# Hybrid GLA and retention decoder step: retention outputs and keys turned by DMA and VectorE instead of TensorE

## The reference, cut to what matters

```python
def _layer(x, pos, s_gla, s_ret, ...):           # 2 layers, x is 2048 x 1024, fp32
    z = rmsnorm(x, norm_w) @ w_in                # one projection, columns split:
    gq, gk, gv, gg, glr, rq, rk, rv, rg = split_cols(z)      # 4 heads, dk 64, dv 128 each group
    la = log_sigmoid(glr @ w2 + b) / 16
    q_b, k_b = rope(rq), rope(rk) * 64 ** -0.5
    o_a, S_gla = gla_chunked(gq * 64 ** -0.5, gk, gv, la)    # S_t = diag(alpha_t) S + k^T v
    o_b, S_ret = ret_chunked(q_b, k_b, rv)                   # S_t = gamma_h S + k^T v
    o_a = rmsnorm_per_head(o_a) * gla_norm_w * silu(gg)
    o_b = (groupnorm_per_head(o_b) * ret_norm_w + ret_norm_b) * silu(rg)
    return x + concat(o_a, o_b) @ w_out
```

## Time and profile before

| | |
|---|---|
| median of 3 runs | 1712.52 us (1712.15 to 1712.91) |
| the profiled execution's own time | 1712.96 us |
| its span, first to last instruction | 1711.2 us |
| PE busy | 1688.4 us (99%), 10154 matmuls |
| DVE, POOL, ACT busy | 975.2, 843.8, 635.9 us |
| chain that ended last | 97% PE, of it 82% line 684 |
| granted TensorE clock | 0.999 |
| DMA | 165470 packets, 215.97 MB, 126 GB/s over the span |

### The profile page before, as it was taken

One profiled execution on the slowest core, in us unless ns is written; L12 is line 12 of the kernel. 1 busy time (PEld: TensorE's weight loads), 2 busy tenths in 40 slices (PEclk: granted clock), 3 DMA queues, 4 the chain that ended last, 5 costly groups with the idle time before them and its releaser, 6 DMA issues.

```text
span 1711.2 us, 26417 instructions
## 1 busy us (share of the span) xinstructions
PE 1688.4 (99%) x10154; PEld 1388.8 (81%) x10154; DVE 975.2 (57%) x2316; ACT 635.9 (37%) x1255; POOL 843.8 (49%) x661
## 2 busy tenths in 40 slices
PE   6999999999999999999999999999999999999998
PEld 4888878888788887888878888788887888878886
DVE  6742576746755275463754436758477454784454
ACT  4433244333343233442342423334234343343322
POOL 3445345554455544464544544547445464454635
PEclk9999999999999999999999999999999999999999
DMA  7412357433542244522454224574245422442224
GB/s 259 138 63 87 99 199 209 138 109 124 181 152 75 87 136 147 131 83 78 154 149 101 74 75 150 177 187 141 75 151 154 118 74 85 141 159 75 87 87 142
DMA packets 165470, 215.97 MB, mean 126 GB/s; under 512 B 80224, under 2 KB 82656, under 8 KB 165344
## 3 DMA queue, kind: packets, MB, share of 16 engines
q10 hardware_dynamic: 73872, 134.51, 24.0%
q1 hardware_dynamic: 91472, 79.77, 16.0%
HBM read 192.34 MB, written 21.89 MB: 125 GB/s over the span
## 4 chain that ended last, share of the span: by engine, by line
PE 97%; DMA 1%; DVE 1%; issue 0%; SPq 0%; ACT 0%; ACTq 0%; POOLq 0%; POOL 0%
PE bank L684 82%; PE bank L959 3%; PE bank L1000 2%; PE bank L965 2%; PE bank L943 1%; PE bank L926 1%; PE bank L747 1%; PE bank L905 1%; PE bank L867 1%; DMA region<-in_x_prompt 1%; PE bank L651 1%; PE bank L909 1%; PE bank L976 0%; PE bank L757 0%; PE bank L884 0%; PE bank L705 0%
## 5 line engine op out<-in xcount | busy, mean ns | idle before, releaser
L266 POOL TENSOR_TENSOR w_lo<-w_stage,w_hi 128x512 fp32r<-128x512 f32 x264 | 360.8, 1388 | 349.2 <-ACT w_hi L259 349.2
L684 PE MATMUL bank<-h_hi,w_hi 128*128 128x512 f32 x1024 | 410.2, 401 | 4.2 <-DVE h_lo L353 4.2
L684 PE MATMUL bank<-h_lo,w_hi 128*128 128x512 f32 x1024 | 400.0, 391 | 0.0
L684 PE MATMUL bank<-h_hi,w_lo 128*128 128x512 f32 x1024 | 399.8, 390 | 0.0
L266 POOL TENSOR_TENSOR w_lo<-ss,w_hi 128x512 fp32r<-128x512 f32 x164 | 218.7, 1354 | 227.8 <-ACT w_hi L259 227.8
L259 ACT ACTIVATE w_hi<-w_stage 128x512 fp32r<-128x512 f32 x264 | 152.6, 624 | 355.2 <-PE bank L684 319.7
L684 PEld LDWEIGHTS bank<-h_hi,w_hi 128*128 128x128 f32 x1024 | 192.5, 188 | 54.2 <-issue 7.2
L684 PEld LDWEIGHTS bank<-h_hi,w_lo 128*128 128x128 f32 x1024 | 192.6, 188 | 41.7
L684 PEld LDWEIGHTS bank<-h_lo,w_hi 128*128 128x128 f32 x1024 | 192.9, 188 | 36.9
L684 PE MATMUL bank<-w_hi,h_hi 128*128 128x512 f32 x512 | 202.6, 396 | 0.3 <-DVE region L1619 0.3
L684 PE MATMUL bank<-w_hi,m_hi 128*128 128x512 f32 x512 | 202.8, 396 | 0.0
(11 more groups left out here) (215 smaller groups left out, 2264.2 us busy)
## 6 DMA issues: line engine op xcount, KB each, us to landing
w_stage<-in_w_slots ACTq DMA_DIRECT2D x264, 256.0 KB, 3.0
ss<-in_w_slots ACTq DMA_DIRECT2D x164, 256.0 KB, 2.9
v_b<-in_w_slots ACTq DMA_DIRECT2D x84, 256.0 KB, 3.0
region<-in_x_prompt SPq DMA_DIRECT2D x32, 512.0 KB, 4.5
xn<-in_x_t SPq DMA_DIRECT2D x16, 512.0 KB, 4.3
out_acts<-region SPq DMA_DIRECT2D x16, 512.0 KB, 3.6
xn<-out_acts SPq DMA_DIRECT2D x128, 64.0 KB, 3.4
region<-out_acts SPq DMA_DIRECT2D x16, 512.0 KB, 3.3
```

Source lines behind the costliest of these rows:

```text
L266: pool.tensor_tensor(w_lo[:, r, c], stage(h), w_hi[:, r, c].bitcast(f32), ALU.subtract).then_inc(lo_done, 1)
L684: i = pe.matmul(P[q][:, :], x, y, start=(s == 0 and kk == 0 and c == 0), stop=(s == 3 and kk == 1 and c == 2), skip_group_check=True)
```

## The change

It takes `keys_natural` and the g = 0 half of `mixed_t` out of TensorE's stream. In their place:

- `turn_outputs` (SP, w = 14): each 128 tokens of normalised `o_n` go to DRAM (`o_rows`, 4 DMAs of 256 KB), and when all four have landed 16 DMAs of 64 KB in runs of 128 bytes bring them back, turned in blocks, into the same buffer (`o_t`). `mixed_ret` (DVE, w = 18) turns the 32x32 blocks with four transposes of 128x512, ACT applies scale and bias in place (w = 18), DVE multiplies by the gate, ACT makes `m_hi` (w = 19) and POOL `m_lo` (w = 19 to 22).
- `turn_keys` (SP, w = 6 and 18): the same for `k_t`, 2 DMAs of 256 KB out to `k_rows` and 16 of 32 KB back into `k_n`; `keys` (DVE) turns the blocks with one transpose of 128x1024, for g = 0 with a multiplication by the decay behind it.
- In blocks 3 to 6 `load_next` moves from w = 4 to 7 to w = 8 to 11, without its wait for TensorE's slot. Waits of TensorE and ACT are adapted: the first wait for `kn_sb` is now that of the states.

The core of the diff (`mixed(g, t)` of DVE loses its g = 0 half; `keys_natural` is gone):

```diff
+            def turn_outputs(n):
+                if n > 0:
+                    sp.wait_ge(ob_in.sem, ob_in.at(n, 0))
+                for t in range(TPB):
+                    sp.wait_ge(normed.sem, normed.at(n, t + 1))
+                    sp.dma_start(d["o_rows"][TOK * t:TOK * t + TOK, :], o_n[:, t, :]).then_inc(or_out.sem, 16)
+                sp.wait_ge(or_out.sem, or_out.at(n, 64))
+                for h in range(HEADS):
+                    runs = d["o_rows"][:, 128 * h:128 * h + 128].rearrange("(c b) (j a) -> j b c a", b=32, a=32)
+                    for j in range(4):
+                        sp.dma_start(o_t[32 * j:32 * j + 32, h, :].rearrange("p (c a) -> p c a", a=32), runs[j]).then_inc(ob_in.sem, 16)
+
+            def turn_keys(n, g):
+                if n > 0 or g == 1:
+                    sp.wait_ge(kb_in.sem, kb_in.at(n, 256 * g))
+                    sp.wait_ge(st_ps.sem, st_ps.at(n, 4 * g))
+                for p in range(2):
+                    sp.wait_ge(qk_gla.sem, qk_gla.at(n, 3 + p)) if g == 1 else sp.wait_ge(rope_st.sem, rope_st.at(n, 4 * p + 4))
+                    sp.dma_start(d["k_rows"][128 * p:128 * p + 128, :], k_t[:, p, :]).then_inc(kr_out.sem, 16)
+                sp.wait_ge(kr_out.sem, kr_out.at(n, 32 * g + 32))
+                runs = d["k_rows"].rearrange("(f b) (t j a) -> t j b f a", b=32, t=TPB, a=32)
+                for t in range(TPB):
+                    for j in range(4):
+                        sp.dma_start(k_n[32 * j:32 * j + 32, t, :].rearrange("p (f a) -> p f a", a=32), runs[t][j]).then_inc(kb_in.sem, 16)
...
-                    if 4 <= w < 8 and n < LAST:
+                    if 4 <= w < 8 and n < NBLK - 1:
                         window(n, w)
                         load_next(n + 1, w - 4)
+                    if 8 <= w < 12 and NBLK - 1 <= n < LAST:
+                        load_next(n + 1, w - 8)
+                    if w in (6, 18):
+                        turn_keys(n, w // 18)
+                    if w == 14:
+                        turn_outputs(n)
...
-                        if 15 <= w < 19:
-                                t = w - 15
-                                g = 4
-                                pool.wait_ge(mhi_sb.sem, mhi_sb.at(n, t + 1))
-                                pool.tensor_tensor(m_lo[:, g:g + 4, TOK * t:TOK * t + TOK], tmp[:, t % 2, :].rearrange("p (h n) -> p h n", h=4),
-                                                   m_hi[:, g:g + 4, TOK * t:TOK * t + TOK].bitcast(f32), ALU.subtract).then_inc(mlo_sb.sem, 1)
+                        if 19 <= w < 23:
+                            h = w - 19
+                            pool.wait_ge(mhi_sb.sem, mhi_sb.at(n, h + 1))
+                            pool.tensor_tensor(m_lo[:, 4 + h, :], o_t[:, h, :], m_hi[:, 4 + h, :].bitcast(f32), ALU.subtract).then_inc(mlo_sb.sem, 1)
...
                     def scores(g, t):
-                        if t == 0:
-                            pe.wait_ge(kn_sb.sem, kn_sb.at(n, 2 * g + 2))
...
                     def state_update(g, t):
+                        if t == 0:
+                            pe.wait_ge(kn_sb.sem, kn_sb.at(n, 2 * g + 2))
...
-                        if w in (7, 19):
-                            keys_natural(w // 19)
...
-                        if 13 <= w < 17:
-                            mixed_t(0, w - 13)
...
+                        if w == 18:
                             for h in range(HEADS):
+                                act.wait_ge(o_turned.sem, o_turned.at(n, h + 1))
+                                nc.scalar.activation(o_t[:, h, :], o_t[:, h, :], ACT.Identity, scale=parh[:, 1 + h:2 + h], bias=parh[:, 5 + h:6 + h]).then_inc(m_aff.sem, 1)
+                        if w == 19:
+                            for h in range(HEADS):
+                                act.wait_ge(mix_sb.sem, mix_sb.at(n, h + 1))
+                                nc.scalar.activation(m_hi[:, 4 + h, :], o_t[:, h, :], ACT.Copy).then_inc(mhi_sb.sem, 1)
...
+                        vec.wait_ge(kb_in.sem, kb_in.at(n, 256 * g + 256))
+                        i = vec.transpose(k_n[:, :, :], k_n[:, :, :])
+                        if g == 1:
+                            i.then_inc(kn_sb.sem, 2)
+                            return
+                        i.then_inc(k_turned.sem, 1)
+                        vec.wait_ge(k_turned.sem, k_turned.at(n, 1))
+                        k4 = k_n[:, :, :].rearrange("p t (h n) -> p t h n", h=HEADS)
+                        vec.tensor_tensor(k4, k4, kdec[:, :].unsqueeze(1).unsqueeze(3).to_broadcast([128, TPB, HEADS, DK]), ALU.mult).then_inc(kn_sb.sem, 2)
...
+                    def mixed_ret():
+                        vec.wait_ge(ob_in.sem, ob_in.at(n, 256))
+                        for h in range(HEADS):
+                            vec.transpose(o_t[:, h, :], o_t[:, h, :]).then_inc(o_turned.sem, 1)
+                        vec.wait_ge(g_silu.sem, g_silu.at(n, 4))
+                        for h in range(HEADS):
+                            vec.wait_ge(m_aff.sem, m_aff.at(n, h + 1))
+                            vec.tensor_tensor(o_t[:, h, :], o_t[:, h, :], g_t[:, h, :], ALU.mult).then_inc(mix_sb.sem, 1)
```

More of the change, by code:

```diff
@@ L182, in build @@
         gate_x = Count(sem("gate_x"), 2)
-        kn_ps, kn_sb = Count(sem("kn_ps"), 4), Count(sem("kn_sb"), 4)
-        att_ps, o_ps, st_ps, mt_ps = (Count(sem(n), 8) for n in ("att_ps", "o_ps", "st_ps", "mt_ps"))
+        kr_out, kb_in, k_turned, kn_sb = Count(sem("kr_out"), 64), Count(sem("kb_in"), 512), Count(sem("k_turned"), 1), Count(sem("kn_sb"), 4)
+        att_ps, o_ps, st_ps = (Count(sem(n), 8) for n in ("att_ps", "o_ps", "st_ps"))
+        mt_ps = Count(sem("mt_ps"), 4)
+        or_out, ob_in, o_turned = Count(sem("or_out"), 64), Count(sem("ob_in"), 256), Count(sem("o_turned"), 4)
         ht_ps = Count(sem("ht_ps"), 8)
@@ L847, in free_bank @@
                             pe.wait_ge(y_add.sem, y_add.at(n, q + 1))
[L849 to L869, removed]
                     def scores(g, t):
@@ L876, in scores @@
                             pe.wait_ge(la_sb.sem, la_sb.at(n, 2))
-                        if t == 0:
-                            pe.wait_ge(kn_sb.sem, kn_sb.at(n, 2 * g + 2))
-                        else:
+                        if g == 1 and t == 0:
+                            pe.wait_ge(qk_gla.sem, qk_gla.at(n, 4))
+                            pe.wait_ge(zt_sb.sem, zt_sb.at(l, 3))
+                        if g + t > 0:
                             pe.wait_ge(att_sb.sem, att_sb.at(n, 4 * g + t))
@@ L937, in scores_pair @@
                             pe.wait_ge(la_sb.sem, la_sb.at(n, 2))
+                        else:
+                            pe.wait_ge(qk_gla.sem, qk_gla.at(n, 4))
+                            pe.wait_ge(att_sb.sem, att_sb.at(n, 4))
+                            if kind == 1:
+                                pe.wait_ge(s_v.sem, s_v.at(l, V_SO[0]))
                         for t in (2 * j, 2 * j + 1):
@@ L977, in state_update, with mixed_t @@
                         i.then_inc(st_ps.sem, 1)
[L979 to L991, removed]
+                    def mixed_t(t):
+                        pe.wait_ge(normed.sem, normed.at(n, 4 + t + 1))
+                        dst = mixed_bank(kind, t)
+                        if kind > 0:
                             pe.wait_ge(att_sb.sem, att_sb.at(n, 8)) if t < 2 else pe.wait_ge(o_sb.sem, o_sb.at(n, 8))
                         elif t < 2:
-                            pe.wait_ge(kn_sb.sem, kn_sb.at(n, 4))
                             pe.wait_ge(sgla_sb.sem, sgla_sb.at(n, 8))
@@ L1039, in body @@
                                 state_update(g, t)
-                        if 13 <= w < 17:
-                            mixed_t(0, w - 13)
                         if w in (25, 26):
-                            mixed_t(1, 2 * (w - 25))
-                            mixed_t(1, 2 * (w - 25) + 1)
+                            mixed_t(2 * (w - 25))
+                            mixed_t(2 * (w - 25) + 1)
                         if w == 27 and n < LAST:
@@ new lines, in mixed @@
+                    def mixed(t):
+                        vec.wait_ge(mt_ps.sem, mt_ps.at(n, t + 1))
+                        if t == 0:
+                            vec.wait_ge(g_silu.sem, g_silu.at(n, 8))
+                        vec.wait_ge(mlo_sb.sem, mlo_sb.at(n, 4 + t - 1 if t >= 2 else 4))
+                        dst = tmp[:, t % 2, :].rearrange("p (h n) -> p h n", h=HEADS)
+                        src = mixed_bank(kind, t)[:, :].rearrange("p (h n) -> p h n", h=HEADS)
+                        vec.scalar_tensor_tensor(dst, src, parh[:, 0:1], g_t[:, :, TOK * t:TOK * t + TOK], ALU.mult, ALU.mult).then_inc(mix_sb.sem, 1)
```

56 lines of the change are left out of this document (12 added, 44 removed).

## The result

The changed kernel took 1684.22 us, median of four runs (1683.29 to 1685.21), against 1712.49 before: a ratio of 0.9835, 95% interval 0.9818 to 0.9852. That is 28.3 us or 1.65% faster. The profiled execution took 1683.42 us, its span is 1681.6.

What follows compares the result with a forecast made beforehand. The prediction took TensorE's instruction stream as the bound: 14.2 us of key and 14.1 of output transposes removed, 28.3 together, nothing added by waits, bring 1712.96 to 1684.7, a median of 1684.2; range 1681.5 to 1700.

Steps and rivals of the forecast that it cites:

- Removed from TensorE: TensorE's stream loses 16 key batches of 0.886 us and 32 output batches of 0.44: 14.2 and 14.1, together 28.3 us.
- Keys of g = 0: Round trip of g = 0 keys: likeliest 16.7 us, range 12.1 to 23.2, against 20.6 available; 4 us in time.
- Outputs: Turned outputs finish by about 566.5, before ACT's high part at 568.86; if later, slot 21's weights suffer. Cost: nothing.
- Keys of g = 1: Second key round trip ends at 575.1, needed at 584.9: 10 us in time. Cost: nothing.
- Engine time: VectorE gets 51 us of new work and loses 32 PSUM copies; it is idle 736 us.
- DMA: Round trips add 33.6 MB in all; about 304,700 packets and 249.5 MB in the changed profile.
- The cover: Weight loads hold beside the new DMA bursts; otherwise each would cost its lateness beyond 8.3 us.
- Layer 1's loads: Moved input loads delay the sample's v in n = 5, issued 1132.5 to 1136.7: at most 1.1 us late, taken as 0.
- The rule against the change: Skill page's 19 times slower strided DMA transpose would make round trips overrun 20 us; judged not to bite on 128-byte runs.
- Late keys: Rival, chance 0.19: g = 0 keys take 21 to 23.2 us, costing 0.5 to 2.6 in eight blocks: 1688 to 1705.
- The slower rival: Chance 0.07: g = 0 key loads in `turn_keys` drain slowly; TensorE waits from 0.66 us each; 1727 at 1.0.

Runs made afterwards that it cites:

- the kernel with the outputs back: The changed kernel with the g = 0 retention outputs turned on TensorE again, keys still by DMA: 1698.78 us.
- the later sets: The changed kernel measured twice more without any edit: 1683.61 us and 1683.86 us.
- keys_32: The changed kernel with the turned keys loaded by 32 DMAs of 16 KB in place of 16 of 32 KB: 1737.14 us.
- x_early: The changed kernel with layer 1's input loads back in slots 4 to 7, before the keys on SP: 1697.22 us.
- x_late: The changed kernel with layer 0's input loads also moved to slots 8 to 11, behind the keys: 1683.03 us.

## Why the prediction was right

Forecast 1684.2 us, measured 1684.22. The mechanism was right; that the two agree to 0.02 us is luck, for some of its sizes and one of its side mechanisms were off.

- **Removed from TensorE.** A batch of eight at 0.886 us came out as 0.90, 14.3 us in all. A batch of four at 0.44 was read too short, from one batch's start to the next matmul's; the slots and the kernel with the outputs back both show 0.47. The term of 14.1 was 15.0 to 15.1, and the spans differ by 29.6 where the sum has 28.3. That the first median shows just 28.3 is partly luck: two of its four executions took 1685; the later sets gained 28.9 and 28.4.
- **Keys of g = 0.** Right in six blocks, wrong in the two that decide. From the end of k's rotation to `k_n` ready it took 16.6 to 17.5 us in n = 0 and 3 to 7, where the sum has 16.7, but 20.1 in n = 2, the block that the sum was made for, and 290.72 - 269.94 = 20.8 in n = 1, against 20.6 of need. The keys were to be 4 us in time in n = 2 and were 0.5. The store was taken at 3.6 and took 2.4 to 4.0 in the other blocks, but 6.7 in n = 1 and 2; the loads of layer 0's input beside it were not in the working. The issues were taken at 0.45 and took 0.49 to 0.59 with their gaps. All this is within the range of 12.1 to 23.2, whose upper end takes 3.4 for the landing although its row goes to 5.1; but the path ended at the edge from which it costs, and that it cost 0.2 us and no more is partly luck.
- **Outputs.** TensorE never waited for them, as forecast. The spare was right in size. With 64 loads they land at 588.4 in n = 2 and TensorE waits 10.2 us from 586.7; so they would have had to land at 578.2, an estimate, 8.5 us before slot 21 was due, where the working had 573.2 against 580.38, 7.2 before. With 32 loads they land 12.1 before it, and nothing waits. What suffers first was wrong: the step named the split of slot 21's weights on ACT, the trace names the copy of GLA's v on ACT, a bank and not a weight.
- **Keys of g = 1.** 10 us in time were forecast, 9.0 to 17.6 measured, 4.6 in n = 5. Nothing lost.
- **Engine time.** VectorE's new work is 51.0 us as summed.
- **DMA.** 249.5 MB is right. Packets are 311,902 where 304,700 were forecast, 7168 more: 448 more DMAs with 16 each, a term that was left out (`keys_32` has 256 more DMAs for the same bytes, and 316,000 packets, 4098 more). The cover held.
- **Layer 1's loads.** The move costs nothing in n = 5, as forecast. The sample's v went out at 1114.6, which with the 19.4 us gained by then is 1134.0 in the time of before: between the 1132.5 and the 1136.7 of the working, of which the latter doesn't follow from its terms (1129 and eight at 0.70 give 1134.6). What the move is worth, 13.5 us, was not worked out.
- **The rule against the change.** The page "VectorE: DVE Perf Modes" of the Trainium skill (section "The three transpose paths") has a plain DMA copy that transposes by strides 19 times slower than the crossbar path, when the innermost stride of the destination is large; as the prediction applied it, the round trips would have overrun. They take up to 20.8 us, and 16 loads of 128-byte runs are issued in 8 and the last lands 3.4 later: as predicted from the row, nothing of that kind shows where 32 floats stay whole. No run here has the crossbar path or a copy with such a stride, so the figure itself wasn't tested.
- **Rivals.** Late keys are the true limit, but at 0.2 us, not 0.5 to 2.6 in eight blocks. The slower rival is real in its mechanism, which `keys_32` shows; but its price was too low, for it took a wait at its own length (38.4 us of waits there, 53.4 of time).

## What to carry to other kernels

When TensorE's stream is the time, a transpose that goes to DMA and another engine is worth the whole time that it occupied, as long as the round trip ends before its use; so work out the reserve block by block, with the other traffic of that block, not once. What stands before a round trip on its queue belongs to the path: here the order of loads on SyncE was worth as much as the keys themselves. Once something is late, look for the next instruction in the waiting engine's own loop, and count more than the wait.

## What the runs showed of the hardware

- A wait of TensorE can cost more than its length. Behind the waits of 3.2 us and more of `x_early` and `keys_32` the granted clock was 0.50 (1.2 GHz) for some microseconds, and each cost 1.4 to 2.8 us beside itself; of two waits of 1.97 us in `keys_32` one cost 0.1 more and the other 1.7.
- The issue time of a DMA on SP goes little by its bytes: 0.43 us for 16 KB, 0.45 for 32, 0.68 for 128, medians of loads in 128-byte runs from DRAM. From SBUF to SBUF 32 KB took 0.61.
- The store of g = 0's keys, 2.4 to 4.0 us in other blocks, took 6.7 in n = 1 and 2 beside 512 KB loads, and 3.3 to 3.5 there when these loads came later (`x_late`).
- A profile's packet count holds more than the data: 16 more for each DMA, by 7168 in the changed kernel.
